# Pooling a normalised token stream before its scale and shift, in a two-block transformer kernel on one Trainium2 core

## What is computed

```python
x = layer_norm(ALPHA * x + g2 * swiglu(modulate(x, sh2, sc2), w_in, w_out), ln_g[0, 1], ln_b[0, 1])   # end of layer 0
hx = x * (1 + sc1) + sh1                    # layer 1: scale and shift per channel, from the condition c
for g, w in enumerate((2, 4, 8, 16)):       # each window w has 256 of the 1024 channels
    pooled_g = (cs[hi] - cs[lo]) / (hi - lo) - hx_g       # a mean over a window of tokens, less the token
y = einsum('bsgi,gio->bsgo', pooled, w_pool) * pool_scale
x = layer_norm(ALPHA * x + g1 * y, ln_g[1, 0], ln_b[1, 0])
x = layer_norm(ALPHA * x + g2 * swiglu(modulate(x, sh2, sc2), w_in, w_out), ln_g[1, 1], ln_b[1, 1])
```

## Time and profile before

| what | value |
|---|---|
| median of 3 runs | 1206.1 us (1205.81 to 1208.53) |
| the profiled execution, its own time | 1208.5 us |
| its span | 1206.7 us |
| PE busy | 1119.9 us, 93% |
| DVE busy | 786.0 us, 65% |
| ACT busy | 491.6 us, 41% |
| POOL busy | 99.8 us, 8% |
| granted TensorE clock, mean | 0.965 of full speed |
| chain that ended last | PE 80%, DVE 9%, ACT 4%, issue 4%, DMA 1% |

### The profile page before, as it was taken

The page is one execution under the profiler, slowest core; times in us unless marked ns, Lnnn a source line. Parts: engine busy times, 40 slices in busy tenths (PEclk is TensorE's granted clock), DMA queues, the critical chain, the costliest instruction groups (busy, mean ns, idle before and its releaser), DMA issues.

```text
span 1206.7 us, 17048 instructions
## 1 busy us (share of the span) xinstructions
PE 1119.9 (93%) x7015; PEld 969.1 (80%) x7015; DVE 786.0 (65%) x1073; ACT 491.6 (41%) x625; POOL 99.8 (8%) x84
## 2 busy tenths in 40 slices
PE   4878999979999999599999989999999988999998
PEld 2665786759999877499998878887777767999987
DVE  2376867768878878777554485569873685555543
ACT  2242433534333332433333365465655534434332
POOL 0000000000000001000000000244656000000000
PEclk9788999899999998899999989999999998999999
DMA  9695462483997787257755536534333343555552
GB/s 337 244 378 210 166 253 70 143 310 115 360 330 275 263 300 257 88 172 258 251 175 196 179 115 202 164 116 140 106 116 129 120 159 121 192 177 177 185 198 105
DMA packets 145135, 236.98 MB, mean 196 GB/s; under 512 B 4901, under 2 KB 86306, under 8 KB 144930
## 3 DMA queue, kind: packets, MB, share of 16 engines
q1 hardware_dynamic: 138128, 221.12, 54.1%
q10 hardware_dynamic: 6930, 14.77, 3.3%
HBM read 229.32 MB, written 6.55 MB: 195 GB/s over the span
## 4 chain that ended last, share of the span: by engine, by line
PE 80%; DVE 9%; ACT 4%; issue 4%; DMA 1%; ACTq 1%; POOL 1%; DVEq 0%; SPq 0%
PE bank L622 77%; PE bank L697 3%; ACT w_hi L1261 2%; DVE ring_lo L1661 2%; DMA ring<-in_ffn_w_out 1%; ACTq L1293 1%; DVE modacc L1782 1%; DVE y_tok L1972 1%; DVE small L1974 1%; POOL ring_lo L2604 1%; DVE y_tok L1970 0%; DMA big<-in_ln_b 0%; DVE small L1861 0%; ACT hc_hi L1321 0%; DVE tmp L1845 0%
## 5 line engine op out<-in xcount | busy, mean ns | idle before, releaser
L1661 DVE TENSOR_TENSOR ring_lo<-ring,w_hi 128x2048 fp32r<-128x2048 f32 (+3 forms) x145 | 325.4, 2245 | 274.4 <-ACT w_hi L1261 274.1
L1261 ACT ACTIVATE w_hi<-ring 128x2048 fp32r<-128x2048 f32 (+3 forms) x157 | 295.0, 1880 | 445.9 <-PE bank L622 412.4
L622 PE MATMUL bank<-h_hi,w_hi 128*128 128x256 f32 x1056 | 302.9, 287 | 5.6 <-DVE h_lo L1680 3.3
L622 PE MATMUL bank<-h_lo,w_hi 128*128 128x256 f32 x1056 | 300.6, 285 | 0.0
L622 PE MATMUL bank<-h_hi,ring_lo 128*128 128x256 f32 x1056 | 300.5, 285 | 0.0
L622 PEld LDWEIGHTS bank<-h_hi,w_hi 128*128 128x128 f32 x1056 | 204.6, 194 | 7.4 <-DVE h_lo L1680 3.9
L622 PEld LDWEIGHTS bank<-h_lo,w_hi 128*128 128x128 f32 x1056 | 204.7, 194 | 1.0 <-issue 1.0
L622 PEld LDWEIGHTS bank<-h_hi,ring_lo 128*128 128x128 f32 x1056 | 204.5, 194 | 0.0
L622 PE MATMUL bank<-w_hi,h_hi 128*128 128x512 f32 (+4 forms) x320 | 127.2, 398 | 11.1 <-DVE h_lo L1908 7.8
L622 PE MATMUL bank<-w_hi,h_lo 128*128 128x512 f32 (+4 forms) x320 | 123.7, 387 | 0.0
L622 PE MATMUL bank<-ring_lo,h_hi 128*128 128x512 f32 (+4 forms) x320 | 123.6, 386 | 0.0
(11 more groups left out here) (269 smaller groups left out, 1446.5 us busy)
## 6 DMA issues: line engine op xcount, KB each, us to landing
aux<-in_w_mod SPq DMA_DIRECT2D x24, 2048.0 KB, 10.1
ring<-in_ffn_w_in SPq DMA_DIRECT2D x88, 512.0 KB, 4.9
ring<-in_w_in SPq DMA_DIRECT2D x24, 1024.0 KB, 5.0
ring<-in_ffn_w_out SPq DMA_DIRECT2D x22, 1024.0 KB, 5.3
ring<-in_w_ffn_in SPq DMA_DIRECT2D x44, 512.0 KB, 4.6
ring<-in_attn_w_qkv SPq DMA_DIRECT2D x12, 1024.0 KB, 13.3
ring<-in_w_ffn_out SPq DMA_DIRECT2D x11, 1024.0 KB, 5.0
bias_rows<-srow ACTq DMA_DIRECT2D x1, 5376.0 KB
```

The source lines that it names most:

```text
L622: return nc.tensor.matmul(o, l, r, start=start, stop=stop, **kw)
L1261: nc.scalar.activation(panel_part(i, 0), raw_panel(i), ACT.Copy).then_inc(w_hi, 1)
L1661: V.tensor_tensor(panel_part(i, 1), raw_panel(i), panel_part(i, 0).bitcast(F32), ALU.subtract)\
```

## The change

Four things change.
- **Pooling of the normalised tokens.** `residual_stats` and `normalise_first` now also serve the passage from `ffn0` to the pooling, so `y_tok` holds the normalised tokens, and PE takes them straight for `pl`. Scale and shift are applied where DVE copies the PSUM result to `pooledT`: scale as a column, shift times the row sums of the pooling matrices, an array `shift_sums` (128x2048) that is made ahead. ACT's copies go. `poolw` waits for four chunks of `pooledT` for each half rather than for all eight.
- **Columns.** Components 6 and 7 come out as columns. `fold_rows` goes, `fold_norm(0, 6, 6)` and one 128x2048 multiplication for `shift_sums` come in its place. The row sums are loaded in one DMA where two bias rows were loaded. `ln_cols` is 8 groups of columns wide, with two more small DMAs at the start.
- **Residual input.** `x_tok` of token tile 0 is rebuilt by POOL (`first_tile_affine`, two operations 128x1024), tile 1 by DVE behind the eight `pl` results; DVE waits for POOL behind its own tile.
- **Order.** The two low splits of `ffn1`'s first panels stand behind DVE's `normalise_second` and behind the fourth of its `lows`. ACT's high split of the first panel stands behind `normalise_first`.

```diff
@@ shape_constants
+    sums = pool.astype(np.float64).sum(1).astype(np.float32)
+    sums = np.repeat(sums, KC // len(POOL_WINDOWS), axis=0).reshape(-1)
@@ tiles
-        mod_rows = v3(big[:, 11264:13312], 2)
+        shift_sums = v3(big[:, 11264:13312], KC)
-        hx_tok = v3(big[:, 0:2048], TT)
...
@@ small loads
-            [(lnsrc[(4 + i) * KC:(5 + i) * KC, :], a[w][1, 1, :].rearrange("(n p) -> n p", p=P))
-             for i, w in enumerate(("ln_g", "ln_b"))]
+            [(lnsrc[(4 + 2 * k + i) * KC:(5 + 2 * k + i) * KC, :], a[w][1 - k, 1, :].rearrange("(n p) -> n p", p=P))
+             for k in range(2) for i, w in enumerate(("ln_g", "ln_b"))]
...
         def mod_is_row(comp):
-            return comp in (2, 5, 6, 7, 8, 11)
+            return comp in (2, 5, 8, 11)
@@ PE
             for kt in range(TT):
-                pe.wait_ge(hx_done, kt + 1)
                 for ch in range(KC):
+                    if ch % PK == 0:
+                        pe.wait_ge(*((xn_done, 3 + ch // PK) if kt else (xn_first, 2)))
...
-                    ins = mm(bank[:, 0:SEQ], hx_tok[:, kt, ch * P:(ch + 1) * P],
+                    ins = mm(bank[:, 0:SEQ], y_tok[:, kt, ch * P:(ch + 1) * P],
                              pool_m[:, kt * 4 + ch // 2, :], kt == 0, kt == TT - 1)
...
-            wait_emptied(pe, ("pl", KC - 1))
             w, = panel(("pool", 0, 0))
             for nb in range(2):
                 for tt in range(TT):
+                    for ch in range(PK * nb, PK * nb + PK):
+                        wait_emptied(pe, ("pl", ch))
@@ ACT
-            for comp in range(2):
-                bias_row(mod_rows[:, comp, :], 1, comp, rows_landed)
+            row_load(big[:, 11264:13312], a["const_pool_sums"], rows_landed)
...
-                if name == "ffn1":
-                    normalise_first(3)
+                if name != "ffn2":
+                    normalise_first({"ffn0": 1, "ffn1": 3}[name])
...
-            for ch in range(KC):
-                empties(nc.scalar.activation(pooledT[:, ch, :], result(act, ("pl", ch))[:, 0:SEQ], ACT.Copy),
-                        ("pl", ch))
@@ DVE, residual_stats
                 V.memset(small[:, 47:48], 0.0).then_inc(used, 1)
+                if stage == "ffn0_out":
+                    mod_finish(10)
                 inverse_root()
@@ DVE, x_from_normalised
-                for tt in range(TT):
+                for tt in tiles:
                     step(V.tensor_tensor(x_tok[:, tt, :], y_tok[:, tt, :], ln_rows[:, 0, :], ALU.mult))
...
+                if len(tiles) < TT:
+                    dve.wait_ge(x_by_pool, 1)
@@ DVE, program
-            for half in range(2):
-                split_to(first + 3 + half)
-                step(fold_rows(half, tmp[:, 0, :]))
-                settle()
+            split_to(first + 3)
+            fold_norm(0, 6, 6)
+            split_to(first + 4)
+            dve.wait_ge(rows_landed, 16)
+            settle()
+            step(V.tensor_tensor(shift_sums, shift_sums, modcol[:, 0, :].unsqueeze(2).broadcast_to([P, KC, SEQ]), ALU.mult))
...
-            pool_gain(0)
-            inverse_root()
-            pool_input(0)
...
-            split_to(last_panel("pool", 0) + 2)
-            for tt in range(TT):
-                step(affine(x_tok[:, tt, :], tt, ln_rows[:, 0, :], ln_rows[:, 1, :]))
...
-            residual_stats("poolw", g1row, g1_used, last_panel("pool", 0) + 1)
+            residual_stats("ffn0_out", g2row, g2_used, last_panel("ffn0_out", 1))
+            for ch in range(KC):
+                empties(V.scalar_tensor_tensor(pooledT[:, ch, :], result(dve, ("pl", ch))[:, 0:SEQ], modcol[:, 1, ch:ch + 1],
+                                               shift_sums[:, ch, :], ALU.mult, ALU.add), ("pl", ch))
+            x_from_normalised(1, tiles=range(1, TT))
+            fold_norm(6, 9, 2)
+            residual_stats("poolw", g1row, g1_used, last_panel("pool", 0))
             lows_and_splits("ffn1_h", last_panel("pool", 0), mod_col(6), mod_col(7))
@@ POOL
+            def first_tile_affine():
+                x = x_tok[:, 0, :]
+                pool.wait_ge(xn_first, 2)
+                pool.wait_ge(ln_landed, 32 * 2)
+                nc.gpsimd.tensor_tensor(x, y_tok[:, 0, :], ln_rows[:, 0, :], ALU.mult).then_inc(x_gained, 1)
+                pool.wait_ge(x_gained, 1)
+                nc.gpsimd.tensor_tensor(x, x, ln_rows[:, 1, :], ALU.add).then_inc(x_by_pool, 1)
...
                     token_root(tt)
+                if stage == "ffn0_out":
+                    first_tile_affine()
```

More of the change, by code:

```diff
@@ L1032, in _ @@
             release(("pool", 0, 0), ins, ("poolw", 1, TT - 1))
-            x_transposes_by_tile("ffn1_h", 1)
+            x_transposes_by_tile("ffn1_h", 2)
             ffn("ffn1")
-            x_transposes_by_tile("z_h", 2)
+            x_transposes_by_tile("z_h", 3)
             dense_w = {}
@@ L1712, in _ @@
                                  ALU.mult))
-            empties(V.tensor_copy(ln_cols, v3(result(dve, "ln_cols")[:, 0:6 * KC], 6)), "ln_cols")
+            empties(V.tensor_copy(ln_cols, v3(result(dve, "ln_cols")[:, 0:8 * KC], 8)), "ln_cols")
             empties(V.tensor_copy(posT[:, :], result(dve, "pos")[:, 0:32]), "pos")
@@ L1793, in mod_finish @@
                         bank = result(dve, ("mod", comp, half))
[L1794 to L1801 removed]
+                        dst = (g1row if comp % 6 == 2 else g2row)[:, cols_]
+                        dve.wait_ge(g_landed[comp % 6], 16 * (comp // 6 + 1))
+                        empties(V.tensor_tensor(dst, bank[:, :], dst, ALU.add), ("mod", comp, half))
                 else:
@@ L2025, in affine, with x_from_normalised @@
                 return V.scalar_tensor_tensor(dst, dst, rstd(tt), bias_row, ALU.mult, ALU.add)
-            def x_from_normalised(ln, signal=None, between=None):
+            def x_from_normalised(ln, signal=None, between=None, tiles=range(TT)):
                 dve.wait_ge(xn_first, xns[0])
@@ L2089, in ffn @@
                         mod_product(HALF_AT[(name, nb)], range(KC // 4))
-            fold_norm(4, 0)
+            fold_norm(4, 3, 0)
             residual_stats("wo", g1row, g1_used, last_panel("wo", 1))
@@ L2117, in _ @@
             mod_product(17, range(2, 4))
-            def pool_gain(tt):
-                step(V.scalar_tensor_tensor(hx_tok[:, tt, :], y_tok[:, tt, :], mean(tt), mod_rows[:, 1, :],
-                                            ALU.subtract, ALU.mult))
-                settle()
-            def pool_input(tt):
-                hx = hx_tok[:, tt, :]
-                V.scalar_tensor_tensor(hx, hx, rstd(tt), mod_rows[:, 0, :], ALU.mult, ALU.add).then_inc(hx_done, 1)
-            split_to(last_panel("ffn0_out", 1))
-            residual_piece("ffn0_out", g2row, 0, 0)
-            residual_piece("ffn0_out", g2row, 0, 1)
-            residual_piece("ffn0_out", g2row, 1, 0)
-            tile_stats(0)
-            pool_gain(0)
-            inverse_root()
-            pool_input(0)
-            residual_piece("ffn0_out", g2row, 1, 1)
-            tile_stats(1)
-            V.memset(small[:, 47:48], 0.0).then_inc(g2_used, 1)
-            pool_gain(1)
-            inverse_root()
-            pool_input(1)
-            mod_finish(10)
-            split_to(last_panel("pool", 0) + 2)
-            for tt in range(TT):
-                step(affine(x_tok[:, tt, :], tt, ln_rows[:, 0, :], ln_rows[:, 1, :]))
-            settle()
-            V.memset(small[:, 47:48], 0.0).then_inc(ln_used, 1)
-            fold_norm(6, 1)
-            residual_stats("poolw", g1row, g1_used, last_panel("pool", 0) + 1)
+            residual_stats("ffn0_out", g2row, g2_used, last_panel("ffn0_out", 1))
[5 more added lines that the diff above has]
+            residual_stats("poolw", g1row, g1_used, last_panel("pool", 0))
             lows_and_splits("ffn1_h", last_panel("pool", 0), mod_col(6), mod_col(7))
```

40 lines of the change are left out of this document (11 added, 29 removed).

## The result

| | before | after |
|---|---|---|
| median on this chip | 1205.8 us (1204.5 to 1208.5) | **1200.1 us** (1194.2 to 1202.2) |
| ratio, 95% interval | | 0.9948 [0.9927, 0.9969] |
| profiled execution, its span | 1208.5, 1206.7 us | 1199.5, 1197.7 us |
| granted TensorE clock, mean | 0.965 | 0.968 |

What follows compares the result with a forecast made beforehand. PE was taken as 80% of the chain of waits, idle 12.32 us behind poolw because DVE was late. Terms -6.8 + 1.4 + 0 = -5.4 us against the 1206.1 median gave 1200.7 us, range 1199.0 to 1204.0 (8 in 10).

Steps and rivals of the forecast that it cites:

- Up to `pl`: 0.: From hx_tok's statistics to PE's start of pl: 3.19 us, start at 475.10 against 475.16, no gain.
- `pl` the same.: PE's 32 pl instructions: 475.1 to 485.0, half clock first as now; second tile's input ready with 4 us to spare.
- Behind `pl`: -6.8.: DVE between pl and the residual pieces behind poolw: pieces start at 488.35, not 495.13, 6.8 us earlier.
- POOL's half: hidden.: POOL's two x_tok operations, 2.5 us each, end near 480.3, 7 us to spare; cost 0, range 0 to 0.6.
- The splits given back: +1.4.: Start of ffn1: the two low splits now stand there as at ffn0's start, costing 1.4 us.
- The sign that was named: Sign of being right: 16.5 to 17 us from the end of normalise_second to ACT's split of ffn1's fourth panel.
- The floor of 1.25: Start of ffn1: least cost in us of the new order of the low splits, whatever the clock.
- The start: 0.: Program start: two more small DMAs, up to 0.7 us, end in 1.0 us of ctx load wait; taken as 0.
- Components 6 and 7: Components made as columns, with the shift_sums work: 1.84 us against 1.88 on PE, costed at 0 in all.
- The first: Rival: part of the gain lost to half clock at ffn1's start or to the program start, 1202.7 to 1203.4; chance 0.24.
- no gain: Rival: poolw's results or DVE's copies so slow that residual pieces start near 494; 1205.5 us; chance 0.07.
- slower: Rival: DVE waits for POOL's x_tok operations, deciding from over 11.5 us each; 1212.1 us at 12; chance 0.04.

Runs made afterwards that it cites:

- six_more_loads: Changed kernel plus six more small unused loads (eight more than before) ahead of the first transposes; 1204.0 us, one run.
- old_moved_between: Kernel before with its two low splits moved, and ffn1's third low split between x_tok's multiplications and additions; 1199.3 us, 0.9948 to before.
- both_in_gap: Changed kernel, but DVE rebuilds both x_tok tiles and folds the columns ahead of its eight pl copies, without POOL; 1198.1 us, 0.9943 to before.
- pool_later: Changed kernel, but POOL starts its two x_tok operations only when normalise_second is done; 1199.9 us, 0.9958 to before.
- A: Not a run: distance in a trace from the end of pl to the start of the first residual piece behind poolw; 10.08 us before, 3.41 after.
- both_behind: Changed kernel, but DVE rebuilds both x_tok tiles behind the eight pl copies, without POOL; 1202.9 us, 0.9975 to before.
- turns: Changed kernel, but DVE folds columns and rebuilds x_tok tile 1 ahead of its copies, then POOL tile 0 beside them; 1196.1 us, 0.9925 to before.
- B: Not a run: distance from the end of normalise_second behind poolw to ACT's high split of ffn1's fifth panel; 21.04 us before, 22.69 after.
- old_splits_moved: Kernel before with only the two low splits of ffn1's first panels moved behind normalise_second and the fourth low; 1200.0 us, 0.9951 to before.
- splits_first: Changed kernel, but the two low splits of ffn1's first panels back ahead of DVE's x_tok tile; 1204.1 us, 0.9990 to before.
- turns_between: As turns, plus ffn1's third low split between x_tok's multiplications and additions; 1197.8 us, 0.9924 to before; run again, 1196.0 us, 0.9924.
- group (2): Kernels run on one chip with one set of runs of the kernel before (median 1207.1 us): changed kernel again, turns, turns_between, six_more_loads.

## Why the prediction was right, and where its reading fell short

- *The number.* 1200.7 us was forecast and 1200.1 measured, within the range of 1199.0 to 1204.0. The medians differ by 5.7 us for a forecast of 5.4, and the distances of the two profiles leave 5.1 to 6.2 us for the change itself, as worked out under `pl`.
- *Up to `pl`: 0.* From the row of the statistics to PE's start of `pl` it is 3.25 us in both (471.91 to 475.16, 470.65 to 473.90), for a forecast of 3.19. Right.
- *`pl` the same.* It took 8.55 us, not 9.9, as the clock rose earlier in it. When the clock rises differs from profile to profile: the changed kernel itself took 8.55 and 8.54 us, and 10.01 in six_more_loads, which has the same passage. That part is luck. But what an early clock brings is part of the change. In the old order `pl` took 9.89, 10.03 and, with the early clock of old_moved_between, still 9.66 us, since PE waits for the second tile's input; in the new order it took 8.55 at that clock, and 7.14 where the clock stayed full. So about 1.1 of the 1.34 us come from the second tile's earlier input, where the clock is early, and the change's own part is 5.1 us at the clock of the profile before and some 6.2 at that of the profile after (an estimate, from one profile of the old order at that clock). The forecast asked only whether the new input comes in time, not whether the old one would with a faster PE.
- *Behind `pl`: -6.8.* 10.08 became 3.41, **-6.67**. The copies took 3.51 us for eight, 0.44 each for a forecast of 0.45, though this is the pace of `pl`'s results: in both_in_gap, where DVE was behind, seven followed one another in 2.82 us, one every 0.40. `x_tok` took 2.5 and marker and `fold_norm` 0.44, as forecast.
- *POOL's half: hidden.* 2.36 and 2.42 us for a forecast of 2.5, over at 478.74 when DVE came to its marker at 485.42. Hidden, with 6.7 us to spare. That `normalise_second` may wait for both was in the range (0 to 0.6) and taken as 0. It did wait, to 479.03, but that was before PE needed it, and pool_later shows the same A without it. The rule of the Trainium skill (SBUF — State Buffer, Who interferes with whom), exclusion for the length of an instruction, holds here: 5.00 us beside POOL and 1.00 without. Its other half holds too: it says that a DVE instruction with at most one SBUF input, outside the 2-port modes, doesn't contend, and the copies, with one tensor from PSUM and one from SBUF, took 0.484 us each beside POOL and 0.484 alone.
- *The splits given back: +1.4.* 1.62 at the fourth panel, 1.65 at the fifth. The sign that was named, 16.5 to 17 us to the fourth panel's split, came out (16.90), but by the half clock of that profile; at full clock it is 15.3 (15.34 in both_behind, 15.33 in six_more_loads), and the order's cost shows at the fifth panel only. The floor of 1.25 from the order alone was too small: with full clock it was 22.79 - 21.04 = 1.75 in both_behind and 1.66 in turns. By the rows of both_behind PE starts the third panel at 518.09, 16.77 us behind `normalise_second`, a little later than the 16.5 at which I had put the end of its low split. That clock and order don't add up was right in the forecast, and B is 22.6 to 23.0 with either.
- *The start: 0.* Right, with more cover than I thought: 1.8 us, PE's idle time, and not 1.0. Components 6 and 7 left no trace either: until the passage the kernels stand 0.2 to 0.6 us apart, but for one load at the end of `ffn0` and the split that I named.
- *The rivals.* The first, 6.7 us of dense work at half clock that lose 3.4 us, came about by half: there were 3.6 us of such work. B grew by 1.65, no more than DVE's late split costs at full clock. The others didn't occur. Two of their figures leave out the 1.4 us given back: with the pieces starting at 494, "no gain" would be near 1206.4 and not 1205.5, and "slower" would begin at POOL operations of some 11 us each and not 11.5; they took 2.4.

**What the sum didn't see.** I worked out when the residual pieces would start in the new order, and that was right. But the sentence on where the 6.8 us come from names two splits of 2.29 and two operations on `x_tok`. These are 4.6 + 2.7 us, and the eight copies of 3.5 came in: 3.8, not 6.8. The missing part is the wait of 4.49 us for ACT's high split, which stood in DVE's timeline and was not among the rows read, less some 1.4 us that DVE in the forecast's new order waits for `pl`'s results (485.45 less eight copies is 481.9, and DVE was free of the splits' place at 480.5). The wait can be removed in two ways: by moving the splits behind the critical work (old_splits_moved), or by taking the copies from ACT, so that its high split comes early (splits_first, where the two splits take 4.48 us in a row). The first also removes the splits themselves; the second brings the copies in. Because of this I credited the change as a whole with what one part does. By the runs: the place of the two splits gives 0.9951 alone, and without it the rest gives 0.9990 [0.9968, 1.0012], though its A and B are 2.6 us shorter in sum. Applied on top of it, the rest of the change moves A from 2.50 to 3.41, the wrong way (what it gains in `pl` at an early clock is outside A), because copies that were ACT's are now DVE's, at the one place where DVE is late. POOL's share, worth 2.41 us by both_behind, makes up for most of that.

**The fastest version.** turns and turns_between take the remaining time from DVE, with ratios of 0.9925 and 0.9924 to the kernel before, the latter twice. On the chip of group (2) the kernel after had 0.9944; the intervals overlap, so that turns beats it rests on A (1.77 for 3.41) and is likely, not settled. That turns_between beats turns is shown by B only (21.10 for 22.70), not by the times. What no run shows: old_moved_between at full clock, where B of the other kernels suggests that it would be as good as turns; and what decides at which moment the clock rises.

## What to carry to other kernels

In a queue that runs in order, look at which instruction waits for something that the ones behind it don't need: here a prefetch for a later stage, two splits ahead of the residual stream, cost 9 us of DVE's time, half of it spent waiting. Move such work behind the last instruction of the critical chain first, alone, and measure that before rewriting what the stage computes. And when a sum comes out, check it a second way, as what went less what came: a difference points to a wait that hasn't been read. A part that takes the same time before and after can also hide a wait, which shows only when its engine gets faster.

## What the runs showed of the hardware that I had not expected

- **The clock and the spread.** Runs of one kernel spread over 3 to 13 us, and mostly go with the mean granted clock: the kernel after had 1194.2 us at 0.975 and 1202.2 at 0.970, turns 1193.2 at 0.976 and 1201.4 at 0.967. The clock rose at another moment of the passage in nearly each profile: `pl` took 7.14, 8.5, 8.8 or 9.9 us in the new order. A part of 2 us can't be read from one span, but distances between two instructions at one clock repeat to 0.01 us (A of the changed passage: 3.41, 3.41 and 3.42).
- **GpSimd holds some of VectorE's operations up fully, and others not at all.** Two normalising operations of 1.00 us in sum took 5.00 beside POOL's 2.36 and 2.42, yet cost the kernel nothing. The copies from PSUM took 0.484 us each with POOL beside them or not.
- **Two causes, one cost.** Half clock alone at the start of `ffn1` cost 1.6 us (old_moved_between), a late low split alone 1.6 to 1.8 (six_more_loads, turns, both_behind), and both together 1.65 to 1.9 (after, pool_later), so that taking away either alone gains nothing when the other is there (old_moved_between).
